# High and low feature halves in one 512-column matmul, summed at eviction, in a two-block model kernel

## The reference, cut to what matters

```python
# first block: mixer, then a sparse feed-forward with 16384 experts
proj = hn @ w_in                      # q, k, v, g, z, xbc, dt, gate_a, gate_b
y_a = gla(...) @ w_up_gla             # up-projection, 1024 x 1024
y_b = ssd(...) @ w_up_ssd             # up-projection, 2048 x 1024
mixed = sigmoid(gate_a) * y_a + sigmoid(gate_b) * y_b
h = h + mixed @ w_out
h = h + peer_ffn(rmsnorm(h))          # top 16 x 8 heads of experts, gathered rows
# second block: retention layer, then stick-breaking attention
h = h + rms_norm(retention(h) @ ret_w_out)
k, v = split(rms_norm(h) @ w_kv)      # "key" is the first 1024 columns of w_kv
h = h + rms_norm(stick_breaking(u @ sb_w_in, k, v) @ sb_w_out)
```

## Time and profile before

| | us |
|---|---|
| median of 3 runs | 1539.13 (1538.02 to 1539.28) |
| profiled execution, its own time | 1537.0 |
| its span in the trace | 1535.2 |
| PE busy, whole span | 1366.7 |
| DVE busy | 1050.0 |
| ACT busy | 693.3 |
| mean granted TensorE clock | 0.966 of full speed |

### The profile page before, as it was taken

How to read it: one execution, slowest core, us unless ns; L and a number is a source line. 1 busy time by engine, 2 the same in 40 slices (tenths; PEclk the granted TensorE clock), 3 DMA queues, 4 the chain that set the end, 5 groups by cost and what they waited for, 6 DMA issues and landing times.

```text
span 1535.2 us, 17810 instructions
## 1 busy us (share of the span) xinstructions
PE 1366.7 (89%) x6585; PEld 982.5 (64%) x6585; DVE 1050.0 (68%) x2081; ACT 693.3 (45%) x1239; POOL 300.5 (20%) x265
## 2 busy tenths in 40 slices
PE   6999989999997987778778777878899999999997
PEld 6989979879996333333323333333497788998876
DVE  5767578776688777777677677665785456755554
ACT  5665677555463322122222222222453465656872
POOL 1000000000023654444444443442100000000000
PEclk9999999999998998999999998989999999999999
DMA  7454454545778999999999999999765456454542
GB/s 247 144 174 129 150 176 141 179 125 178 278 290 341 418 422 421 422 421 421 422 421 422 421 422 421 421 421 422 282 209 163 123 182 201 160 171 138 159 147 79
DMA packets 77798, 417.65 MB, mean 272 GB/s; under 512 B 8768, under 2 KB 8832, under 8 KB 44688
## 3 DMA queue, kind: packets, MB, share of 16 engines
q0 software_dynamic: 36864, 268.45, 42.3%
q1 hardware_dynamic: 40848, 148.06, 29.8%
HBM read 415.39 MB, written 1.08 MB: 271 GB/s over the span
## 4 chain that ended last, share of the span: by engine, by line
PE 53%; DMA 27%; DVE 12%; ACT 5%; issue 2%; POOL 1%; DVEq 0%; SPq 0%; POOLq 0%; ACTq 0%
DMA SLAB<-in_peer_uv,C 20%; PE ps L1024 12%; PE ps L1026 12%; PE ps L1025 12%; PE ps L1311 8%; DMA AR<-in_peer_uv,C 6%; DVE wlo L1889 2%; DVE SLAB L2206 1%; DVE AR L2206 1%; ACT whi L1477 1%; PE ps L1245 1%; DVE AR L2050 1%; POOL SLAB L2438 1%; POOL AR L2438 1%; ACT AR L1684 1%
## 5 line engine op out<-in xcount | busy, mean ns | idle before, releaser
L1889 DVE TENSOR_TENSOR wlo<-raw,whi 128x1024 fp32r<-128x1024 f32 x246 | 299.4, 1221 | 161.0 <-ACT whi L1477 160.2
L1477 ACT ACTIVATE whi<-raw 128x1024 fp32r<-128x1024 f32 x246 | 258.6, 1056 | 119.2 <-PE ps L1026 108.8
L1311 PE MATMUL ps<-AR 128*128 128x512 f32 x508 | 247.9, 641 | 69.7 <-ACT AR L1684 67.0
L1024 PE MATMUL ps<-XH,whi 128*128 128x256 f32 (+1 forms) x1032 | 300.4, 291 | 5.7 <-DVE AR L2050 1.8
L1311 PE MATMUL ps<-SLAB,AR 128*128 128x512 f32 x516 | 250.9, 641 | 59.9 <-ACT AR L1684 59.4
L1026 PE MATMUL ps<-XH,wlo 128*128 128x256 f32 (+1 forms) x1032 | 293.3, 284 | 0.0
L1025 PE MATMUL ps<-XL,whi 128*128 128x256 f32 (+1 forms) x1032 | 293.0, 284 | 0.0
L2438 POOL DMA_INDIRECT AR<-in_peer_uv,C x127 | 148.3, 1168 | 608.4 <-DVE C L1869 429.0
L1311 PEld LDWEIGHTS ps<-AR 128*128 128x128 f32 x508 | 101.7, 206 | 213.6 <-issue 114.6
L1311 PEld LDWEIGHTS ps<-SLAB,AR 128*128 128x128 f32 x516 | 103.2, 205 | 205.2 <-issue 121.1
L2206 DVE CUSTOM_DVE_ANT_0 SLAB<-SLAB,AR 128x1024 f32<-128x1024 f32 x129 | 156.8, 1223 | 74.3 <-DMA SLAB<-in_peer_uv,C 74.1
(11 more groups left out here) (377 smaller groups left out, 1478.5 us busy)
## 6 DMA issues: line engine op xcount, KB each, us to landing
raw<-in_stream SPq DMA_DIRECT2D x246, 512.0 KB, 3.7
AR<-scr SPq DMA_DIRECT2D x8, 512.0 KB, 5.5
AR<-in_stream SPq DMA_DIRECT2D x7, 512.0 KB, 8.1
SLAB<-in_peer_uv,C POOLq DMA_INDIRECT x129, 28.2
AR<-in_rows SPq DMA_DIRECT2D x4, 512.0 KB, 5.2
SLAB<-in_stream SPq DMA_DIRECT2D x4, 512.0 KB, 8.7
AR<-in_peer_uv,C POOLq DMA_INDIRECT x127, 28.0
AR<-in_con SPq DMA_DIRECT2D x1, 1280.0 KB, 7.0
```

The source lines that it names most:

```text
L1024: pe.matmul(o, sh, mh, start=first, stop=False)
L1311: t = pe.matmul(ps[2 * i + half][:, :], d, rows_in[:, 512 * half:512 * half + 512], start=c == 0, stop=c == 127)
L1477: a.activation(whi[i % NS][:, :], src, ACT.Copy).then_inc(*hi.up(i))
L1889: v.tensor_tensor(wlo[i % NS][:, :], src, whi[i % NS][:, :].bitcast(F32), ALU.subtract).then_inc(*lo.up(i))
```

## The change

Four kinds of T chunks with 256 moving columns (gates, ya, yb, key) no longer run three matmuls for a k-step but two: one of 512 columns that multiplies `whi` with the XH columns and the XL columns side by side (a two-piece moving operand, 4224 columns apart), into the whole bank, and one of 256 columns, `wlo` with XH, onto the first half. The eviction then has to add the two halves of the bank. DVE does it with a tensor_reduce over pairs of columns 256 apart: for a gate into GA or GB, from which ACT then takes the tanh in place; for ya and yb into a new buffer HALF, before the old multiply; for key straight into KS, in place of ACT's copy. The bank is now freed by the reduce.

```diff
-        XH = in_slab("XH", 2 * NS * CH, XW)
-        XL = in_slab("XL", 2 * NS * CH + XW, XW)
+        features_hl = in_slab("XHL", 2 * NS * CH, 2 * XW)
+        XH, XL = features_hl[:, 0:XW], features_hl[:, XW:2 * XW]
+        XHL = features_hl[:, :].rearrange("p (a c) -> p a c", a=2)
...
+            side_by_side = {"gx": [T * k + NM for k in range(8)], "ya": [8 * T + TX * k for k in range(8)], "yb": y_at,
+                            "key": [TX * k for k in range(8)]}
...
-                    m = triple(ps[b][:, 0:n], whi[i % NS][:, ws], wlo[i % NS][:, ws], xh, xl, k == 0, last)
+                    if what in side_by_side and n == TX:
+                        c = side_by_side[what][k]
+                        wide = XHL[:, :, c:c + TX]
+                        if k:
+                            pe.matmul(ps[b][:, 0:TX], wlo[i % NS][:, ws], xh, start=False, stop=False)
+                        m = pe.matmul(ps[b][:, :], whi[i % NS][:, ws], wide, start=k == 0, stop=last)
+                        if k == 0:
+                            pe.matmul(ps[b][:, 0:TX], wlo[i % NS][:, ws], xh, start=False, stop=False)
+                    else:
+                        m = triple(ps[b][:, 0:n], whi[i % NS][:, ws], wlo[i % NS][:, ws], xh, xl, k == 0, last)
...
                 elif step == "gate":
                     f, i, b = at
-                    on.wait_ge(*prod.of((i, 1)))
-                    on.wait_ge(*dve.of(("nat", 1, 1)))
-                    a.activation((GA if f < 8 else GB)[:, f % 8, :], ps[b][:, 0:TX], ACT.Tanh, scale=0.5).then_inc(*act.up(("gate", f)))
+                    on.wait_ge(*dve.of(("gate_sum", f)))
+                    gate = (GA if f < 8 else GB)[:, f % 8, :]
+                    a.activation(gate, gate, ACT.Tanh, scale=0.5).then_inc(*act.up(("gate", f)))
...
+                elif step == "gate":
+                    f, i, b = at
+                    on.wait_ge(*prod.of((i, 1)))
+                    on.wait_ge(*act.of("eGn"))
+                    v.tensor_reduce((GA if f < 8 else GB)[:, f % 8, :], ps[b][:, :].rearrange("p (a t) -> p t a", a=2), AX.X, ALU.add).then_inc(*dve.up(("gate_sum", f)))
...
                     on.wait_ge(*act.of(("gate", f)))
-                    v.scalar_tensor_tensor(GA[:, f, :], GA[:, f, :], 1.0, ps[b][:, 0:TX], ALU.add, ALU.mult).then_inc(*dve.up(("ya", f)))
+                    on.wait_ge(*dve.now())
+                    v.tensor_reduce(HALF, ps[b][:, :].rearrange("p (a t) -> p t a", a=2), AX.X, ALU.add).then_inc(*dve.up(("ya_sum", f)))
+                    on.wait_ge(*dve.now())
+                    v.scalar_tensor_tensor(GA[:, f, :], GA[:, f, :], 1.0, HALF, ALU.add, ALU.mult).then_inc(*dve.up(("ya", f)))
...
-                    a.copy(KS[:, f, :], ps[b][:, 0:TX]).then_inc(*act.up(("key", f)))
...
+                    v.tensor_reduce(KS[:, f, :], ps[b][:, :].rearrange("p (a t) -> p t a", a=2), AX.X, ALU.add).then_inc(*dve.up(("key", f)))
```

More of the change, by code:

```diff
@@ L922, in build @@
         ZS = place("ZS", 20944, 1024).rearrange("p (b c) -> p b c", b=2)
+        HALF = place("HALF", 512, 256)
         DY = place("DY", 0, 512).rearrange("p (b i c) -> p b i c", b=2, i=2)
@@ L1189, in tensor_program @@
                     f, i, b = at
-                    free[b] = act.of(("gate", f))
+                    free[b] = dve.of(("gate_sum", f))
                 elif step == "bn":
@@ L1249, in tensor_program @@
                     f, i, b = at
-                    free[b] = dve.of(("ya", f))
+                    free[b] = dve.of(("ya_sum", f))
                 elif step == "z_silu":
@@ L1264, in tensor_program @@
                     f, i, b = at
-                    free[b] = dve.of(("yb_gate", f))
+                    free[b] = dve.of(("yb_sum", f))
                 elif step == "out_add":
@@ L1395, in tensor_program @@
                     f, i, b = at
-                    free[b] = act.of(("key", f))
+                    free[b] = dve.of(("key", f))
                 elif step == "spread_roots":
@@ L1778, in scalar_program @@
                     root("h2", RH)
-                elif step == "key":
-                    f, i, b = at
-                    on.wait_ge(*prod.of((i, 1)))
-                    a.copy(KS[:, f, :], ps[b][:, 0:TX]).then_inc(*act.up(("key", f)))
                 elif step == "v2_copy":
@@ L2127, in vector_program @@
                     on.wait_ge(*act.of(("gate", 8 + f)))
-                    v.scalar_tensor_tensor(GB[:, f, :], GB[:, f, :], 1.0, ps[b][:, 0:TX], ALU.add, ALU.mult).then_inc(*dve.up(("yb_gate", f)))
+                    on.wait_ge(*dve.now())
+                    v.tensor_reduce(HALF, ps[b][:, :].rearrange("p (a t) -> p t a", a=2), AX.X, ALU.add).then_inc(*dve.up(("yb_sum", f)))
+                    on.wait_ge(*dve.now())
+                    v.scalar_tensor_tensor(GB[:, f, :], GB[:, f, :], 1.0, HALF, ALU.add, ALU.mult).then_inc(*dve.up(("yb_gate", f)))
                     on.wait_ge(*dve.now())
@@ L2351, in vector_program @@
                     root("h2", RH, D)
+                elif step == "key":
+                    f, i, b = at
+                    on.wait_ge(*prod.of((i, 1)))
+                    v.tensor_reduce(KS[:, f, :], ps[b][:, :].rearrange("p (a t) -> p t a", a=2), AX.X, ALU.add).then_inc(*dve.up(("key", f)))
                 elif step == "spread_roots":
@@ L2366, in vector_program @@
                     ks = KS[:, h:h + 2, :]
-                    on.wait_ge(*act.of(("key", h + 1)))
+                    on.wait_ge(*dve.of(("key", h + 1)))
                     on.wait_ge(*dve.of("spread_roots"))
```

## The result

The change makes the kernel slower: 1556.02 us median of 4 runs (1555.25 to 1556.93), beside 1539.2 (1538.02 to 1540.63, 4 runs) for the kernel before. The ratio is 1.0101, with a 95% interval of 1.0089 to 1.0113, so +16.8 us, where the prediction had +9.0, 1548.1 us, and 1556 as the upper end of its range. The profiled execution took 1556.55 us, its span is 1554.7.

The account below looks back on a forecast made before the run. An ACT-DVE loop was taken to bound the kernel from 158.88 to 209.74 us, PE after 209.7. Terms 0.3 + 10.5 + 1.5 - 3.0 - 0.3 = +9.0 on 1539.1 gave 1548.1 us, range 1540 to 1556.

Parts of the forecast that it names:

- the first loop: ACT-DVE loop before line 1223: each gate's tanh waits for DVE's sum; five gates make PE 10.5 us later.
- gates 0 to 5: Before 158.88 us: DVE's sum delays a gla_state by some 0.9 us, against 0.65 us gained on PE; +0.3.
- Gate 10: Chunk 48 in the loop: the sum waits behind the first of two decay_cb multiplies on DVE; +1.85 us.
- bn 2: Transposes in stage gx: PE must wait 3.9 us for DVE's oT, beside the loop's delay and not in addition.
- the sum itself: DVE's new tensor_reduce at each changed eviction: 0.66 us from its start to its dependent's, 40 of them, 26 us.
- rival C: Slower: strided reduce 1.2 us, DVE bound 240 to 290 us, or operand eats PE's saving; 1551 to 1555; chance 0.22.
- PE's gain: All changed stages: 13.8 ns for each of 384 k-steps, 347.4 in place of 361.2 ns; 5.3 us at most.
- after 209.7 PE sets the pace: From 209.7 us to the end of ya PE idles 0.04 of 78.90 us, so a delay there is paid in full.
- term of +1.5: Gates 12 to 15 and ya: DVE's added 7.9 us of sums costs between 0 and 7.9; +1.5 taken.
- ya and key: ya gains 0.9 us on PE; key gains 0.9, but its last sum delays DVE's roots, leaving -0.3.
- Rival A: Faster: PE sets the pace in gx also, ACT's idle time covers the tanh's wait; 1534.3 us; chance 0.08.
- Rival B: No change: the loop pays only its five sums, 3.3 us, without queueing behind wlo; 1539.4 us; chance 0.15.

Follow-up runs that it names:

- e3: Kernel before, all matmuls as before, with a plain DVE copy put between gate product and ACT's tanh; 1555.18 us, ratio 1.0095.
- e4: Changed kernel with ACT's gate tanh made a step of its own, one eviction later, all sums kept; 1537.58 us, ratio 0.998.
- e11: Changed kernel with gates 12 to 15 as before, plus unread matmuls ahead of bn 2 and the first ssd_state; 1550.58 us, ratio 1.0075.
- e1: Kernel before with the gates alone changed, ya, yb and key as before; 1556.8 us, ratio 1.0114.
- e2: Kernel before with ya, yb and key changed, the gates as before; 1540.11 us, ratio 0.9999.
- e6b: Changed kernel with gates 6, 7, 8, 10 and 11 (chunks 40, 42, 44, 48, 50) as before; 1547.42 us, ratio 1.0044.
- e8b: Changed kernel with unread 512-column matmuls keeping PE busy in three of its waits; 1557.4 us, ratio 1.0112.
- e9: Changed kernel with gates 12 to 15 (chunks 52 to 58) as before; 1553.78 us, ratio 1.0078.
- e7b: Kernel before with all wide matmuls but the old evictions, reading only the first half of the bank, no sums; 1537.86 us, ratio 0.9984.
- e12: Kernel before with the gate tanh one eviction later and side-by-side matmuls in yb alone; 1536.02 us, ratio 0.9973.
- e5b: Kernel before with the gate tanh one eviction later, no matmul wide; 1537.57 us, ratio 0.9989.

## Why the prediction was off, point by point

**Right: the first loop.** The prediction had PE's first ssd_state 10.8 us late (0.3 + 10.5); it was 10.7. At chunk 40 PE is 2.4 us later than before, 1.3 of them from before anything changed, so gates 0 to 5 cost 1.1 and not 0.3. From there the two `silu`s of the rows are 3.9 us late after gate 7 and 6.4 after gate 8, for 3.95 and 6.55 predicted, and the small DMA starts 8.8 us later than in the earlier trace rows, so again 6.4. Gate 10 then cost 1.1 in place of 1.85 (its `silu` at 209.62, before at 199.69), and gate 11 the predicted 2.1. The loop alone is 9.6 for 10.5. That 10.8 and 10.7 agree so well is in part luck: the two small misses cancel. PE waits at bn 2:

```profile
179.11 0.68 PE L1211 MATMUL ps<-C,AR 128*128 128x128 f32 x4 [3.79 <-DVE XHL L2049]
```

3.79 us for the 3.9 that stood in the prediction. e3 and e4 show that the reason is the right one: the place in ACT's queue of a tanh that waits for DVE.

**Right: the sum itself.** The groups of after (busy us, mean ns):

```profile
L2066 DVE TENSOR_REDUCE AR<-ps 128x256 f32<-128x512 f32 x16 | 10.9, 680 | 0.8 <-PE ps L1090 0.7
L2147 DVE TENSOR_REDUCE AR<-ps 128x256 f32<-128x512 f32 x8 | 5.5, 689 | 1.5 <-PE ps L1090 1.2
L2376 DVE TENSOR_REDUCE AR<-ps 128x256 f32<-128x512 f32 x8 | 5.5, 682 | 0.0
```

The sum out of PSUM in steps of 256 columns takes 680 to 689 ns, the contiguous one of the earlier trace rows 686. The part of rival C that rested on a stride at half rate is gone.

**Nearly right: PE's gain.** In key, the last matmul of a chunk's first k-step comes at these times (PE timeline, first and last of eight):

```profile
1336.81 0.28 PE L1092 MATMUL ps<-XHL,wlo 128*128 128x256 f32 x1
...
1356.41 0.28 PE L1092 MATMUL ps<-XHL,wlo 128*128 128x256 f32 x1
```

Seven chunks of eight k-steps in 19.60 us, 350.0 ns for one, where it was 361.2 (3 x 120.4) and the forecast 347.4. A k-step gives 11.2 ns, not 13.8. The Trainium skill, page "TensorE: Matmul & The Clock Gate", section "Back-to-back issue gap", would have it at 2.5, by a formula that it gives for single matmuls without the weight loads between them; the trace disagrees with that as before, by a factor of more than four. yb's 128 k-steps come to 1.4 us; the table shows 1.0 to 1.3, for 1.8 predicted.

**Wrong: "after 209.7 PE sets the pace", and its term of +1.5.** This is the step that failed. The prediction read the earlier trace rows as two stretches with a border at line 1223: a loop ahead of it, PE behind it. For gates 12 to 15 and ya it gave the sums' DVE time between 0 and 7.9 us and took 1.5, less 1.2 for PE's gain there (0.3 and 0.9), so +0.3 from the first ssd_state to z. Measured: +7.5. Of these 7.0 are there before ya starts, and 0.5 come in ya. e11 gives the four gates 6.5 of the 7.0, and e1, where ya is as before, has 7.3. The DVE time was not the thing to bound. The order of steps that cost 1.85 to 2.6 us for a gate of the first loop (DVE's earlier steps ahead of the sum, the tanh ahead of `silu` and `whi` in ACT's queue) is the same for gates 12 to 15, and 6.5 / 4 = 1.6 for a gate is of that size. That PE was gapless in the kernel before says only that the loop had been no slower than PE; the earlier trace rows has no number for the margin, and the prediction treated the missing number as a small cost. Rival C named nearly this place ("DVE becomes the bound from 240 to 290 us") and priced it 6.4 us higher, but with DVE's load as the mechanism. That is not shown: e4 has the same sums at the same DVE load, and its third ssd_state is not late.

**Wrong in a small way: ya and key.** ya was to gain 0.9 on PE and loses 0.4 to 1.2 instead, from its start to z, in after, e2, e4, e6b, e8b, e9 and e11. In e7b, with the wide matmuls and no sum, it gains 0.6. So it is the sums that turn the sign, and the trace of after shows a place:

```profile
302.29 1.12 PE L1250 MATMUL ps<-AR 128*128 128x512 f32 x2 [0.82 <-DVE AR L2094]
```

PE waits 0.82 us for a DVE product that has ya's sums ahead of it in DVE's queue. The same matmul waits 0.75 to 0.87 us in the other six, and has no wait in the kernel before and in e7b. The prediction had named these waits and had no number for them. For key the sum was -0.3. PE's gain of 0.7 (64 x 11.2 ns) is there, but the wait at its end grows by 1.3 (0.70 in the earlier trace rows to 2.02 above), net +0.6: the last sum stands ahead of the roots, as predicted, and costs twice what was put down for it (0.6).

**The sum again**, predicted and in the trace: first loop 10.8 and 10.7; from there to z 0.3 and 7.5; yb -1.8 and -1.0; key and behind it -0.3 and 1.0. Together 9.0 and 18.2 (16.8 by the medians). One term holds 7.2 of the 9.2 us of difference. The measured time stands at the upper end of the stated range, and the range reached so far only for rival C, whose mechanism isn't what the runs show; that much of it is luck.

Rival A (faster) fell with the first loop, and e7b is what it described: no wait for a sum, 0.16% faster. Rival B, which had 3.3 us in the loop, fell with the first ssd_state, 9.6 us in the loop and 9.9 by e6b.

## What to carry to other kernels

An engine without gaps shows only that the others keep up with it, not by how much. Before a step is put between two engines in a stretch that looks bound by a third, ask whether it is the same queue order that bound the stretch before; if so, its price per step holds there too until the margin is known. And when an eviction gets a second engine, move its last part out of the way of the queue's other work: one eviction later made 1556 us into 1537.6 here, and what the side-by-side form paid in the end it paid where nobody waits for the sum (yb), about 1 us of 1540.

## What the chip showed that was not expected

**The clock.** In the kernel before, the granted clock is 1.00 in all of stages gx and ya. After, it falls to half, 1.2 GHz in place of 2.4, in three spells, each behind a wait of PE. Windows around them:

```profile
179.00:184.00 5.00, 4.89 (x24) 4.42 (x25) 4.58 (x8) 2.79 (x5) 0.00 (x0) 0.66 0.44 125
```

```profile
221.00:224.00 3.00, 2.29 (x3) 0.79 (x4) 3.00 (x7) 0.52 (x2) 0.00 (x0) 0.50 0.63 213
224.00:229.00 5.00, 5.00 (x22) 4.38 (x22) 4.70 (x8) 2.74 (x4) 0.00 (x0) 0.66 0.34 111
```

```profile
261.50:264.80 3.30, 3.30 (x17) 3.30 (x17) 3.30 (x6) 2.43 (x4) 0.00 (x0) 0.51 0.23 94
```

Slower matmuls in these spells are part of why PE is busy longer than before with 384 fewer. The waits ahead of them were 3.79 us (bn 2), 4.57 (the first ssd_state) and only 1.54 (the second). A wait's length alone doesn't decide it. Before line 1223 the kernel before waited 2.53 us and its clock stayed at 1.00 (210 to 216 us); e7b, with a wait of 2.53 us at the same matmul, went to half for 6 us, and 2.8 us more delay stands in its column of the table. e12 and e5b have the same wait of 2.64 us at the same place; 1.4 us after it e12's matmuls fall to half pace, up to 205.4, and e5b's don't:

```profile
200.46 0.36 PE L1035 MATMUL ps<-XHL,whi 128*128 128x256 f32 x1 [2.64 <-ACT AR L1601]
...
202.01 1.05 PE L1237 MATMUL ps<-C,AR 128*128 128x128 f32 x4
```

```profile
200.60 0.35 PE L1033 MATMUL ps<-XH,whi 128*128 128x256 f32 x1 [2.64 <-ACT AR L1588]
...
202.06 0.60 PE L1224 MATMUL ps<-C,AR 128*128 128x128 f32 x4
```

The same wait at the same place can thus be followed by a spell, at a cost of 1 to 3 us, or not, and single profiles of these kernels can't be compared more closely than that where a spell lies between. What else decides it is open. Between the first two ssd_state the spell costs 2.5 us where PE sets the pace (e9 against e11) and nothing where the loop does (after against e8b). The unread matmuls took away the spells behind bn 2 and the first ssd_state in e8b and e11, but not every one: the clock is 0.66 from 201 to 206 us in e11 and from 203 to 208 in e8b, and e8b has the one at 262 to 268.6 us, behind a wait of 2.38.
